# Decoder layer on one Trainium2 core: the first two pairs of FFN weight units multiplied chunk by chunk while the conditioning weights land

## What is computed

```python
def _swiglu(h, wg, wu, wd):
    return (jax.nn.silu(h @ wg) * (h @ wu)) @ wd

ada = (jax.nn.silu(c) @ w_ada + b_ada).reshape(c.shape[0], 3, 3, D_MODEL)   # 9 rows of c
mod(t, i)     = t * (1.0 + ada[:, i, 1, None, :]) + ada[:, i, 0, None, :]
post(t, y, i) = _layernorm(DEEPNORM_ALPHA * t + ada[:, i, 2, None, :] * y, ln_g[i], ln_b[i])
x = post(x, 0.5 * _swiglu(mod(x, 0), f1g, f1u, f1d), 0)     # D_FF = 2816
m, st = mixer(mod(x, 1));  x = post(x, m, 1)                # attention and convolution
x = post(x, 0.5 * _swiglu(mod(x, 2), f2g, f2u, f2d), 2)
```

## Time and profile before

| | us |
|---|---|
| median of 3 runs | 867.71 |
| lowest, highest | 867.45, 868.11 |
| the profiled execution | 866.49 |
| its span, first to last instruction | 864.4 |
| from the span's start to the first matmul of the FFN | 38.54 |
| from there until pairs 0 and 1 and four slabs are through PE | 32.35 |

### The profile page before, as it was taken

One profiled execution on the slowest core, in us unless ns is written; L12 is line 12 of the kernel. 1 busy time (PEld: TensorE's weight loads), 2 busy tenths in 40 slices (PEclk: granted clock), 3 DMA queues, 4 the chain that ended last, 5 costly groups with the idle time before them and its releaser, 6 DMA issues.

```text
span 864.4 us, 16835 instructions
## 1 busy us (share of the span) xinstructions
PE 826.8 (96%) x6708; PEld 736.5 (85%) x6708; DVE 465.7 (54%) x711; ACT 341.6 (40%) x473; POOL 254.6 (29%) x309
## 2 busy tenths in 40 slices
PE   5999999999999999999988989989999999999997
PEld 3799999998899899887665656559799999999996
DVE  0654434434335678536797797449844444444454
ACT  2432333333123585455344333355753333332240
POOL 2030000000002308999999999101100000000030
PEclk9999999999999999999999999999999999999998
DMA  9996786784945435347998999999444444645421
GB/s 300 348 364 229 266 289 223 270 290 158 329 136 178 160 123 195 99 146 236 379 355 286 356 364 361 349 357 377 134 145 148 146 146 146 177 135 161 144 74 61
DMA packets 159601, 197.44 MB, mean 228 GB/s; under 512 B 11907, under 2 KB 132985, under 8 KB 159525
## 3 DMA queue, kind: packets, MB, share of 16 engines
q1 hardware_dynamic: 150445, 187.94, 65.7%
q10 hardware_dynamic: 8800, 8.43, 3.0%
q0 software_dynamic: 288, 0.14, 0.1%
HBM read 193.67 MB, written 3.17 MB: 228 GB/s over the span
## 4 chain that ended last, share of the span: by engine, by line
PE 81%; DVE 8%; DMA 5%; ACT 2%; issue 2%; POOL 1%; SPq 0%; DVEq 0%; ACTq 0%; POOLq 0%
PE bank L1744 19%; PE bank L1746 19%; PE bank L1745 19%; PE bank L2033 5%; PE bank L2058 3%; PE bank L1705 2%; PE bank L2142 2%; DVE kT L1470 2%; DMA araw<-in_w_ada 1%; DMA xrow<-in_x_sample 1%; DMA raw<-in_ffn_wg 1%; DMA araw<-in_cache_v 1%; PE bank L1776 1%; DVE yT L1397 1%; DVE wlo L1156 1%
## 5 line engine op out<-in xcount | busy, mean ns | idle before, releaser
L1156 DVE TENSOR_TENSOR wlo<-raw,whi 128x2048 fp32r<-128x2048 f32 (+1 forms) x80 | 184.1, 2302 | 222.4 <-ACT whi L768 222.2
L1744 PE MATMUL bank<-mh,whi 128*128 128x320 f32 x816 | 254.5, 312 | 0.0
L1746 PE MATMUL bank<-mh,wlo 128*128 128x320 f32 x816 | 252.2, 309 | 0.0
L1745 PE MATMUL bank<-ml,whi 128*128 128x320 f32 x816 | 252.2, 309 | 0.0
L768 ACT CAST whi<-raw 128x2048 fp32r<-128x2048 f32 (+1 forms) x80 | 148.6, 1858 | 202.4 <-PE bank L1746 196.1
L1744 PEld LDWEIGHTS bank<-mh,whi 128*128 128x128 f32 x816 | 153.3, 188 | 5.9 <-issue 5.8
L1745 PEld LDWEIGHTS bank<-ml,whi 128*128 128x128 f32 x816 | 153.3, 188 | 0.1
L1746 PEld LDWEIGHTS bank<-mh,wlo 128*128 128x128 f32 x816 | 153.3, 188 | 0.0
L1744 PE MATMUL bank<-hh,whi 128*128 128x320 f32 x352 | 109.6, 311 | 0.0
L1745 PE MATMUL bank<-hl,whi 128*128 128x320 f32 x352 | 108.8, 309 | 0.0
L1746 PE MATMUL bank<-hh,wlo 128*128 128x320 f32 x352 | 108.8, 309 | 0.0
(11 more groups left out here) (308 smaller groups left out, 1072.2 us busy)
## 6 DMA issues: line engine op xcount, KB each, us to landing
araw<-in_w_ada SPq DMA_DIRECT2D x24, 1024.0 KB, 6.6
raw<-in_ffn_wg SPq DMA_DIRECT2D x22, 1024.0 KB, 9.1
raw<-in_ffn_wu SPq DMA_DIRECT2D x22, 1024.0 KB, 10.4
raw<-in_ffn_wd SPq DMA_DIRECT2D x16, 1024.0 KB, 5.4
raw<-in_cache_k SPq DMA_DIRECT2D x56, 256.0 KB, 4.5
raw<-in_cache_v SPq DMA_DIRECT2D x42, 256.0 KB, 7.1
raw<-in_w_in SPq DMA_DIRECT2D x10, 1024.0 KB, 5.3
raw<-in_w_ada SPq DMA_DIRECT2D x8, 1024.0 KB, 11.2
```

What stands on the lines that cost most here:

```text
L1156: dve.tensor_tensor(wl(slot_w(phase, u))[:, 0:size], landed(phase, u)[:, 0:size], wh(slot_w(phase, u))[:, 0:size].bitcast(F32), ALU.subtra ...
L1744: pe.matmul(bank[:, b, 0:T], wh(slot)[:, c], h_, start=(start and n == 0), stop=False)
L1745: pe.matmul(bank[:, b, 0:T], wh(slot)[:, c], l_, start=False, stop=False)
L1746: ins = pe.matmul(bank[:, b, 0:T], wl(slot)[:, c], h_, start=False, stop=(stop and n == len(parts) - 1))
```

## The change

Early units land in three places of their own (`aland`), apart from the ring, so that the first four FFN units can land between them; these come as **quarters** of two chunks, 256 KB each (`load_piece`, `PIECES`, `STAGES` = 4). Two more split buffers (`whi3`, `wlo3`) let all four units be held split at once (`EARLY` = 4). ACT and DVE split quarter by quarter (`hi_piece`, `lo_piece`). On PE, `early_stage(pair, s)` multiplies the two chunks of quarter s for all targets of a pair, pair 0 into banks 0 to 3, pair 1 into 4 to 6; the target that would need bank 7 comes last (`early_rest`), since bank 7 holds the early conditioning results. An early product is now 32 matmuls of 32 x 64 in place of 8 of 32 x 256; DVE turns it (`early_turn`) with a 32 x 32 transpose, and the ACT copies, the PE turns and 4 of the 5 groups of `keep_clock_early` in their old places go; new groups of 8, 8 and 4 stand after products 0, 1 and 3. The tokens are loaded and turned first. No slab is multiplied in pairs 0 and 1 any more; four more go to the down phase (`ADA_HOSTS` at units 4, 6, 8 and 10). POOL's `fold` is cut in two, the second half behind the first norm.

```diff
-UP1, DN1, WIN, WOUT, UP2, DN2 = (0, 8, 22), (22, 30, 12), (34, 42, 10), (44, 50, 4), (48, 54, 22), (70, 76, 12)
+UP1, DN1, WIN, WOUT, UP2, DN2 = (0, -4, 22), (22, 18, 12), (34, 30, 10), (44, 38, 4), (48, 42, 22), (70, 64, 12)
+PIECES = [(0, 0), (1, 0), (0, 1), (1, 1), (2, 0), (3, 0), (2, 1), (3, 1), (0, 2), (1, 2), (2, 2), (3, 2)]
-ADA_HOSTS = {1: 30, 2: 31}
+ADA_HOSTS = {1: 26, 2: 27, 4: 28, 6: 29, 8: 30, 10: 31}
...
             def load_ada(a, a_, g=0):
                 if a_ >= ADA0 + 2:
                     sp.wait_ge(ada_used, a - 1)
+                else:
+                    sp.wait_ge(w_used, 3)
...
+            load_early_ada(0)
+            load_early_ada(1)
+            for u, s in PIECES[0:2]:
+                load_piece(u, s)
+            load_early_ada(2)
+            load_early_ada(3)
+            for u, s in PIECES[2:8]:
+                load_piece(u, s)
+            load_early_ada(4)
+            load_early_ada(5)
+            for u, s in PIECES[8:12]:
+                load_piece(u, s)
+            load_early_ada(6)
+            load_early_ada(7)
+            for u in range(EARLY):
+                load_piece(u, STAGES - 1)
...
+            def early_turn(u):
+                dve.wait_ge(ada_used, u + 1)
+                q = 2 * QG * (u % 4)
+                turned = rows[:, u // 4, q:q + 2 * QG]
+                dve.transpose(turned, bank[:, 7, 2 * QG * u:2 * QG * u + 2 * QG]).then_inc(early_flip, 1)
+                dve.wait_ge(early_flip, u + 1)
+                at = 2 * ADA_ORDER[u]
+                dve.tensor_tensor(adaT[:, at:at + 2, :], turned.rearrange("p (n r) -> p n r", r=QG)[:, :, 0:9],
+                                  par1[:, at:at + 2].unsqueeze(2).to_broadcast([P, 2, 9]), ALU.add).then_inc(ada_out, 1)
...
+            def ada_product(u):
+                pe.wait_ge(aland_in[u % ADA_LAND], 16 * (u // ADA_LAND + 1))
+                if u:
+                    pe.wait_ge(early_flip, u)
+                slab = aland[:, u % ADA_LAND, :].rearrange("p (k n q) -> p k n q", k=NCH, n=2)
                 for kk in range(NCH):
+                    for g in range(4):
+                        q = slice(QG * g, QG * g + QG)
+                        ins = pe.matmul(bank[q, 7, ...], cT[:, kk, :], slab[:, kk, :, q],
+                                        start=kk == 0, stop=kk == NCH - 1)
...
+            def early_product(target, kk):
+                b, slot, cc, done = target
+                c = slice(UC * kk + P * cc, UC * kk + P * cc + P)
+                pe.wait_ge(mh_ready, kk + 1)
+                pe.wait_ge(ml_ready, kk + 1)
+                pe.matmul(bank[:, b, 0:T], wh(slot)[:, c], mh[:, kk, :], start=kk == 0, stop=False)
+                pe.matmul(bank[:, b, 0:T], wh(slot)[:, c], ml[:, kk, :], start=False, stop=False)
+                return pe.matmul(bank[:, b, 0:T], wl(slot)[:, c], mh[:, kk, :], start=False, stop=kk == NCH - 1)
+            turn_x()
+            turn_params()
+            ada_product(0)
+            keep_clock_early(8)
+            ada_product(1)
+            keep_clock_early(8)
+            early_stage(0, 0)
+            ada_product(2)
+            ada_product(3)
+            keep_clock_early(4)
+            early_stage(0, 1)
+            early_stage(1, 0)
+            ada_product(4)
+            early_stage(1, 1)
+            ada_product(5)
+            early_stage(0, 2)
+            ada_product(6)
+            ada_product(7)
+            early_stage(1, 2)
+            early_last(0)
+            early_last(1)
+            early_rest()
```

More of the change, by code:

```diff
@@ L228, in slot_w @@
         return 1 + u
+    if phase[0] == UP1[0] and u < EARLY:
+        return u
     return u % SLOTS
@@ L241, in slot_before @@
         return (WOUT[0] + 1, WOUT[0] + 2, WOUT[0] + 3, UP2[0])[u]
+    if phase[0] == UP1[0] and u < 6:
+        return u - EARLY
     return phase[0] + u - SLOTS
@@ L524, in load_first_up @@
             def load_first_up(pair, pair_, g):
-                for x in range(2):
-                    load_ada(ADA0 + 2 * pair + x, ADA0 + 2 * pair_ + x, g)
+                if pair_ >= ADA_UP:
+                    for x in range(2):
+                        load_ada(ADA0 + 2 * (pair - ADA_UP) + x, ADA0 + 2 * (pair_ - ADA_UP) + x, g)
                 if pair_ < 9:
@@ L718, in _ @@
             pool.memset(qo[:, :, :, :], 0.0).then_inc(q_zero, 1)
+            fold(1)
             pool.wait_ge(st_in, 2)
@@ L825, in body @@
                             act.wait_ge(hr, 2 * pair + cc - 1)
-                        act.activation(tmp[:, cc, :], bank[:, cc, 0:T], ACT.Silu).then_inc(sr, 1)
-                    if ffn == 0 or pair_:
-                        hi_next(2)
-                    hi_next(3)
+                        act.activation(tmp[:, cc, :], bank[:, first_bank(ffn, pair_) + cc, 0:T], ACT.Silu).then_inc(sr, 1)
+                    if ffn == 0 and pair_ < 2:
+                        if pair_ == 0:
+                            hi_next(4)
+                            hi_next(5)
+                    else:
+                        if pair_:
+                            hi_next(2)
+                        hi_next(3)
                     for cc in range(2):
@@ L1735, in _, with early_targets @@
-            ada_turn(ADA0 - 1, ADA0 - 1)
-            keep_clock_early(6)
+                    pe.matmul(bank[:, 6, 0:P], ident, ident, start=True, stop=True)
+            def early_targets(pair):
+                return [(4 * pair + 2 * x + cc, 2 * pair + x, cc, ((g_ready, u_ready)[x][0], w_used)[cc])
+                        for x in range(2) for cc in range(2) if (pair, x, cc) != (1, 1, 1)]
+            def early_product(target, kk):
[6 more added lines that the diff above has]
+                return pe.matmul(bank[:, b, 0:T], wl(slot)[:, c], mh[:, kk, :], start=False, stop=kk == NCH - 1)
@@ new lines, in early_stage, with early_last @@
+            def early_stage(pair, s):
+                pe.wait_ge(piece_lo, PIECES.index((2 * pair + 1, s)) + 1)
+                for kk in (2 * s, 2 * s + 1):
+                    for target in early_targets(pair):
+                        early_product(target, kk)
+            def early_last(pair):
+                targets = early_targets(pair)
+                for x in range(2):
+                    pe.wait_ge(w_lo, 2 * pair + x + 1)
+                    for kk in (NCH - 2, NCH - 1):
+                        for target in targets[2 * x:2 * x + 2]:
+                            ins = early_product(target, kk)
+                            if kk == NCH - 1:
+                                ins.then_inc(target[3], 1)
@@ new lines, in early_rest @@
+            def early_rest():
+                pe.wait_ge(ada_out, ADA0)
+                for kk in range(NCH):
+                    ins = early_product((7, 3, 1, w_used), kk)
+                ins.then_inc(w_used, 1)
+            pe.wait_ge(c_silu, 1)
+            turn_x()
[7 more added lines that the diff above has]
+            ada_product(3)
```

282 lines of the change are left out of this document (141 added, 141 removed).

## The result

| | before | changed |
|---|---|---|
| median, us | 867.79 (10 runs) | 873.63 (10 runs) |
| lowest, highest | 865.19, 869.42 | 869.95, 877.94 |
| span of the profiled execution | 864.4 | 870.9 |
| mean granted clock of the profiled execution | 0.992 | 0.989 |

The ratio is 1.0072, with a 95% interval from 1.0054 to 1.0090: the change costs 6.2 us, where I forecast 2.8. The direction was right, the size was off by more than a factor of two; the median, 873.6, lies just inside the range, whose upper end is 874.0.

A forecast was written before the change was run, and what follows sets the result against it. Before pair 2 PE is fed by a chain through DVE: product 1 ends at 18.1, plus 48.8 gives 66.9 against 66.8 (+0.1); clock falls add 2.7. Against the 867.71 median: 870.5 us, range 866.3 to 874.0.

The forecast's parts named there:

- The yardstick: Moment when pair 2 can start: 70.89 before, less 4.1 us for four slabs moved behind it, so 66.8 to beat.
- (a): From product 1 to the first `ml` on DVE: 3.9 us, fillers covering 2.1, PE idle 1.8.
- (b): Stage (0,0) on PE, 24 matmuls: 3.5 us.
- (d): From product 3 to `ml` of chunk 2: 2.8 us, four fillers covering 1.0, PE idle 1.7.
- (g): Before stage (0,2), DVE prepares chunks 4 and 5 after product 5: 3.9 us, PE idle throughout.
- (i): DVE's work from product 7 through unit 0's last quarter: 4.0 us, stage (1,2) hiding 2.6, PE idle 1.4.
- (j): Last step to pair 2: PE's 66 matmuls, 9.7 us, against unit 4's load, unit 5, casts and Silu, 11.7; the later counts.
- rival C: Small matmuls dear: 1.36 us per early product in place of 0.95, 2.9 us on the chain, so 873.4; chance 0.08.
- Part 4: Clock falls in PE's gaps before pair 2: 1.2 us for the longest, 1.5 for three borderline ones; sum +2.7 us.
- The cover behind pair 2: Slack before pair 2's up half needs unit 5's low part, slowed by `scale_x`: some 0.4 us; if gone, up to 1.
- A: Rival, neutral: the clock holds through PE's gaps before pair 2; -0.1 to +1.5 us, 868.2; chance 0.23.
- B: Rival, transfers alone decide: pair 2 starts at 56 against 66.8, so 857; chance 0.12 including its half, 862 to 865.

The follow-up runs named there:

- the kernel with one filler group: Changed kernel plus only 13 dummy matmuls on PE after product 5, in the longest idle spell; 870.65 us, ratio 1.0039 to the kernel before.
- the two cures together: Changed kernel plus 13 dummy matmuls after product 5 and the last quarters split ahead of chunks 6 and 7; 865.98 us, ratio 0.9989.
- the kernel with five fills: Changed kernel plus dummy matmuls in the five idle spells of PE before pair 2; 871.43 us, ratio 1.0056.
- the reordered one: Changed kernel with work reordered on SP, PE, ACT and DVE, PE work beside each DVE chain, no fillers after product 3; 860.78 us, ratio 0.9916.
- the one with fillers moved: The reordered one without 8 dummy matmuls after product 0, with 14 after product 1, and product 2 behind stage (0,0); 861.05 us, ratio 0.9931.
- the wide products: Probe: the reordered one with each early product as 8 matmuls of 32 x 256, not 32 of 32 x 64, sums incomplete; 859.19 us, ratio 0.9924.

## Why the prediction was wrong

**The yardstick and the bound** held. Moving four slabs behind pair 2 makes 66.8 the moment to beat; PE is the bound behind it in both kernels.

**The steps from product 1 on** held within a few tenths. Product 1 ended at 17.9 (I said 18.1). With the loss by the clock taken out, (a) measured 3.85 against 3.9, (b) 3.6 against 3.5, (c) and (d) 5.3 against 5.2, (e) 6.3 against 6.2, (f) 4.9 against 4.5, (g) 3.9 against 3.9, (h) 6.2 against 5.9, (i) 3.9 against 4.0, (j) 12.6 against 11.7. The sum is 1.8 us over mine, half of it in (j), and as product 1 ended 0.2 early, pair 2 would have started 1.6 late without the clock. In (j) unit 5 had landed 9.5 us after unit 4's load was issued, not 8.3. SP issued four loads within 3 us; at 292 GB/s, 2.8 MB had been moved by then, where units 4 and 5 are 2.1, so I put the delay down to the later loads in the same queues. A product took 1.03 (start to start, 13.80 to 14.83), not 0.95; the rival C had put it at 1.36. "TensorE: Matmul & The Clock Gate", Back-to-back issue gap (the Trainium skill), with its floor of some 25 ns for each small matmul would make it 1.6; 64 records in 1.03 are 16 ns each, so the measurement decides against that here.

**Part 4, the clock, is the step that failed.** I had +2.7 and it was 5.9 in the trace. Of the 3.7 us by which the trace lies above my 2.8, the clock is 3.2 and the chain 1.6, and by luck the rest of the kernel gave 1.1 back. The mechanism was right and its size was not, for three reasons. First, the gap in (g) was counted as one fall of 3.4 us; the clock stayed down for 6.8, and all but 0.9 us of that was work: 2.75 lost, not 1.2. That it stays down for 6.8 is not certain: the kernel with unit 4 freed early shows the same 6.8 behind the same spell of 3.84, the kernel without the first fillers 3.4 behind one of 3.85. Second, the gaps of (a), (d) and (i) were put at half a chance each and at 1.2, which makes 1.8 and not the 1.5 that I wrote; the one of 1.86 us fell, at 1.6, and those of 1.54 and 1.03 did not. Third, and this is the plain mistake, step (j) contains a gap of its own. Its two ways are 9.7 and 11.7 us long, so PE must idle 2.0 us before pair 2, and Part 4 does not mention it. It measured 2.67 and brought a fall of 1.5. With my own list of spells and the prices measured since, 1.5 for those of 1.8 and 2.0 us and 2.7 for (g), the sum would have been 5.7; that is hindsight for the prices, but not for the missing spell.

Over all runs the picture is the same: the mean granted clock was 0.987 over ten runs of the changed kernel and 0.992 over 29 runs of the one before. Half a per cent of 871 us is 4.4 us more lost to the clock, an estimate, since this mean counts stretches in which PE idled too. That it was cause and not company is shown by the kernel with one filler group, 2.9 us, and by the two cures together, 7.2 us, more than the 6.2 that the change had cost.

**The cover behind pair 2** I put at 0.4 us; by my own numbers, 66 + 6.6 against 66.9 + 7.0, it was 1.3. In the changed kernel unit 5's low part took 7.07 us beside `scale_x` and PE did not wait. In the two kernels that filled spells and freed nothing, DVE's next work did make PE wait, 0.7 and 0.8 us, near the price of 1 us that I had given.

**The rivals.** A, neutral, is what the kernel with both cures does (0.9989), so it was a rival about the clock and the last load only. B, transfers alone decide, was out of reach for this order, as said, for the reason given there: nothing stands on PE between product 5 and stage (0,2). Put work there and 8.2 us come back; carried through, 13.5. C fell: a product took 1.03 us, not 1.36.

**The marks that I set** came out in the main: the longest spell is 3.84 us and stands before stage (0,2), no quarter's DMA ends one, two falls fill three slices of 3.4 us between 20 and 54. Of the four spells that I said DVE would end, ACT ended one (1.54 us, its cast of `mh`), and a fifth stood right before pair 2. Unit 4's load was issued at 60.25 and not 56, and pair 2 started at 72.90 and not 67 to 70, both late mostly by the clock: the two falls before it are 4.35 us.

## What to carry to other kernels

When a change puts an engine's work behind a chain through another engine, list every place where the first one must idle, those at the end of a race between two ways too, and price each spell as its own length plus what the clock takes from the work behind it; here that was as much as half of the idle time again (5.9 us on 11.9 of spells). Before filling such a gap with matmuls that nobody reads, look for work that can stand beside the chain: the same instructions less five fillers, in another order, were worth 13.5 us (1.0072 to 0.9916). A load that waits for a buffer hangs on the last reader of that buffer in program order, so what frees it belongs ahead of anything with a later deadline.

## What the hardware showed that I had not expected

PE pauses by itself while the DMA queues are full. In the kernel with five fills it stood 1.37 us after record 57 of product 3. In the one with products 4 to 7 moved, whose program has 12 filler records fewer ahead of that, it stood 0.56 us five records behind the 64 of product 3, which is record 69 = 57 + 12: the same instruction.

```profile
29.49 0.60 PE L1816 MATMUL bank<-con 128*128 128x128 f32 x3 [0.56 <-issue]
...
38.26 0.65 PE L1779 MATMUL bank<-aland,cT 128*32 128x64 f32 x32 [1.54 <-issue]
```

Both pauses ended at 29.5 to 29.8 whenever PE had come there. The second stands in the middle of product 5 there, and in the kernel with the products moved and unit 4 freed early as well:

```profile
39.82 0.65 PE L1779 MATMUL bank<-aland,cT 128*32 128x64 f32 x32 [1.27 <-issue]
```

The distance from one pause to the next is even, too. Between its two pauses PE has 123 matmul records in the kernel with products 4 to 7 moved (29.48 to 38.26), 124 in the reordered one (38.93 to 45.05), and 124 in the one with fillers moved (40.08 to 46.01), each with as many weight loads. And the last has one filler, two records, fewer in front, and both its pauses come two records later in the order of the work. The page counts an instruction queue of 49 packets and 0.80 MB for the changed kernel, 16 KB each, 46 with the wide products and in the kernel before. I read this as PE's instructions arriving in blocks through queues that weight loads had filled; the places, the even distance and the count agree with it, and the landing of a block itself is not in the trace. "Trainium Architecture — The Big Picture", The software stack (the Trainium skill), has the instruction streams moved to the engines when the program is loaded; by the packets in the profile, part of it happens during the run. A product of 32 small matmuls costs PE no more time than one of 8 wide ones (1.10 against 1.09), but four times the instructions, and it was in such products, or at most some twenty matmuls behind them, that PE paused.

The moment at which the clock first rises is not fixed either. Product 0 took 1.10 us in the changed kernel and 1.94 in the reordered one, though both issue the same instructions up to there.
